# State-space mixer: the two directions' decays added before one masked product, with dt as a logarithm in the exponent

## What is computed

```
dt = softplus(dt_raw + dt_bias)           # per position, direction and head
log_a = dt * -exp(a_log)
v_f, v_b = xh * dt_f, xh * dt_b
# in a chunk, j the position written, l the position read, cs = cumsum(log_a):
y_intra = sum_l (q_j . k_l) * exp(cs_j - cs_l)[j >= l] * v_l      # forward; backward alike with j < l
y_inter = (q_j . h) * exp(cs_j)           # h: the state that the other chunk leaves
y = y_forward + y_backward + xh * d_skip
y = rms_norm_by_group(y * silu(z)) * norm_g @ w_out
```

## Time and profile before

| what | value |
|---|---|
| median of 3 runs | 1048.15 us (1047.29 to 1057.39) |
| profiled execution | 1050.53 us |
| its span, first to last instruction | 1048.7 us |
| mean granted TensorE clock | 0.987 of full speed |
| PE busy | 999.6 us, 95% |
| POOL busy | 693.2 us, 66% |
| ACT busy | 621.7 us, 59% |
| DVE busy | 490.1 us, 47% |

### The profile page before, as it was taken

How to read it: one execution, slowest core, us unless ns; L and a number is a source line. 1 busy time by engine, 2 the same in 40 slices (tenths; PEclk the granted TensorE clock), 3 DMA queues, 4 the chain that set the end, 5 groups by cost and what they waited for, 6 DMA issues and landing times. The chain is left out here.

```text
span 1048.7 us, 16332 instructions
## 1 busy us (share of the span) xinstructions
PE 999.6 (95%) x6297; PEld 879.0 (84%) x6297; DVE 490.1 (47%) x996; ACT 621.7 (59%) x1143; POOL 693.2 (66%) x548
## 2 busy tenths in 40 slices
PE   5999999999999889999999899999989999999988
PEld 4898779999999788988878799999977887787776
DVE  3745344435344466686744544444353143223453
ACT  7636656555546676686766664554565558755621
POOL 3977617765677686677667657575679756766654
PEclk9999999999999999999989999999999999999989
DMA  9774415765554565653744455646445755544311
GB/s 330 237 205 161 132 72 185 249 229 199 180 184 134 162 204 151 211 177 105 241 136 160 146 171 191 201 161 201 162 161 178 193 161 183 181 140 140 110 52 41
DMA packets 131947, 178.71 MB, mean 170 GB/s; under 512 B 21457, under 2 KB 94045, under 8 KB 131677
## 3 DMA queue, kind: packets, MB, share of 16 engines
q1 hardware_dynamic: 127693, 169.95, 50.3%
q10 hardware_dynamic: 4176, 7.71, 2.1%
HBM read 176.51 MB, written 5.24 MB: 173 GB/s over the span
## 5 line engine op out<-in xcount | busy, mean ns | idle before, releaser
L509 POOL TENSOR_TENSOR wlo<-raw,whi 128x512 fp32r<-128x512 f32 x512 | 671.9, 1348 | 331.5 <-ACT whi L1180 325.1
L526 PE MATMUL PS<-Th,whi 128*128 128x256 f32 (+2 forms) x1016 | 290.4, 286 | 3.5 <-DVE Tl L1699 2.8
L528 PE MATMUL PS<-Th,wlo 128*128 128x256 f32 (+2 forms) x1016 | 287.2, 283 | 0.0
L527 PE MATMUL PS<-Tl,whi 128*128 128x256 f32 (+2 forms) x1016 | 287.1, 283 | 0.0
L1180 ACT ACTIVATE whi<-raw 128x1024 fp32r<-128x1024 f32 (+1 forms) x149 | 156.0, 1047 | 178.9 <-PE PS L528 128.1
L523 PE MATMUL PS<-whi,Th 128*128 128x512 f32 (+1 forms) x512 | 206.5, 403 | 10.1 <-DVE Tl L1699 4.2
L1772 DVE SCALAR_TENSOR_TENSOR arena<-PS,cols,arena 128x255 f32<-128x255 f32 (+1 forms) x272 | 118.7, 478 | 189.4 <-ACT arena L1309 165.6
L526 PEld LDWEIGHTS PS<-Th,whi 128*128 128x128 f32 (+2 forms) x1016 | 194.5, 191 | 9.6 <-issue 5.6
L525 PE MATMUL PS<-whi,Tl 128*128 128x512 f32 (+1 forms) x512 | 199.3, 389 | 0.0
L524 PE MATMUL PS<-wlo,Th 128*128 128x512 f32 (+1 forms) x512 | 199.2, 389 | 0.0
L527 PEld LDWEIGHTS PS<-Tl,whi 128*128 128x128 f32 (+2 forms) x1016 | 194.5, 191 | 1.7 <-issue 0.7
(11 more groups left out here) (228 smaller groups left out, 1076.3 us busy)
## 6 DMA issues: line engine op xcount, KB each, us to landing
raw<-in_ffn_w_up_dram SPq DMA_DIRECT2D x44, 1024.0 KB, 5.1
raw<-in_ffn_w_down_dram SPq DMA_DIRECT2D x22, 1024.0 KB, 4.9
raw<-in_w_in_dram SPq DMA_DIRECT2D x22, 1024.0 KB, 5.0
raw<-in_c_w_in_dram SPq DMA_DIRECT2D x16, 1024.0 KB, 5.4
raw<-in_ab_w_in_dram SPq DMA_DIRECT2D x14, 1024.0 KB, 6.2
raw<-in_c_w_out_dram SPq DMA_DIRECT2D x8, 1024.0 KB, 5.3
raw<-in_ab_w_out_dram SPq DMA_DIRECT2D x4, 1024.0 KB, 4.9
raw<-in_c_w_in_dram SPq DMA_DIRECT2D x8, 512.0 KB, 5.4
```

The lines of the kernel that those rows point to most:

```text
L509: i = nc.gpsimd.tensor_tensor(wlo[n % NLO][:, c:e], raw[n % NRAW][:, c:e], whi[n % NHI][:, c:e].bitcast(F32), ALU.subtract)
L526: mm(o, wh, ah, start=first, stop=False)
L527: mm(o, wh, al, start=False, stop=False)
L528: return mm(o, wl, ah, start=False, stop=last)
```

## The change

One product does for both directions. Written as j and l above, forward and backward exclude each other, so the two decays can be added first, and x can stay without dt once log(dt) is in the exponent. In particular:

- `lnd` is the logarithm of dt, clamped at 1e-37 (one VectorE and one ScalarE instruction more, at the start). `ncs`, the bias of the exponentials, was minus the sum and becomes `lnd` minus the sum: four VectorE instructions where ScalarE had one.
- `vx` is x alone, 2 copies a group, in place of `vfb`, 4 products a group.
- The forward exponentials go to `ef` in SBUF, the backward ones to banks 4 and 5. `masked` runs for 4 units w (chunk and half) instead of 8: an add in the bank, then the product.
- `diag` runs for 4 units: 16 products a group instead of 32. Those of chunk 0 stand between slots 3 and 4, those of chunk 1 after slot 4. `T_lo` of the group before is waited for ahead of chunk 0.
- The turned result goes to banks 6 and 7 in every group, and slot 3 waits no more for its reading.
- SyncE issues the rows of units 4 to 7 all ahead of slot b + 7 (6 and 7 were ahead of b + 8), and GpSimd selects them all ahead of slot b + 5 (6 and 7 were ahead of b + 6).
- ScalarE's order changes: units 0, 2, then `T_hi`, 1, 3, the centre tap of the next group's `xs` without the slot that followed it, 4, 5, one slot, 6, 7, then Silu; the next slot comes after Silu.
- VectorE's order follows, with the convolution of the next group ahead of units 2 and 3.

```diff
-            for u, k, m in ((0, 5, 4), (2, 5, 4), (4, 7, 5), (6, 8, 6)):
+            for u, k, m in ((0, 5, 4), (2, 5, 4), (4, 7, 5), (6, 7, 5)):
...
         def turn_bank(g):
-            return 0 if g < SG - 2 else 6
+            return 6
...
-                def diag(u):
-                    c, r, hf = u // 4, (u // 2) % 2, u % 2
-                    pe.wait_ge(*at("s_m", (g, u)))
+                def diag(w):
+                    c, hf = w // 2, w % 2
+                    pe.wait_ge(*at("s_m", (g, w)))
                     for k in range(4):
                         h = 4 * hf + k
-                        i = mm(PS[:, 7 - c, h * DH:(h + 1) * DH], dec[u % 2][:, k, :], vfb[:, r, c, h * DH:(h + 1) * DH],
-                               start=u % 4 == 0 and k == 0, stop=False, skip_group_check=True)
+                        i = mm(PS[:, 7 - c, h * DH:(h + 1) * DH], dec[w % 2][:, k, :], vx[:, c, h * DH:(h + 1) * DH],
+                               start=w % 2 == 0 and k == 0, stop=False, skip_group_check=True)
...
-                pair(0)
-                ssd_slot(g + 1, 3, mid=lambda: pair(2))
-                pair(4)
+                def tile_diag(c):
+                    if g and not c:
+                        pe.wait_ge(*at("T_lo", (("y", g - 1), 3)))
+                    diag(2 * c)
+                    diag(2 * c + 1)
+
+                ssd_slot(g + 1, 3)
+                tile_diag(0)
+                ssd_slot(g + 1, 4)
+                tile_diag(1)
                 if last:
-                    ssd_slot(g + 1, 4)
-                    pair(6)
                     ssd_slot(g + 1, 5, mid=lambda: last_turn(0))
                     last_turn(1)
-                else:
-                    ssd_slot(g + 1, 4, mid=lambda: pair(6))
...
-                    if u >= 2:
-                        act.wait_ge(*at("s_m", (g, u - 2)))
+                    if c:
+                        act.wait_ge(*at("s_m", (g, hf)))
                     for k in range(4):
                         a = ncs_at[(c, r)] + 8 * g + 4 * hf + k
-                        i = act.activation(PS[:, 4 + u % 2, k * P:(k + 1) * P], crow[v % 4][:, k, :], ACT.Exp, bias=ncs[:, a:a + 1])
+                        o = PS[:, 4 + hf, k * P:(k + 1) * P] if r else ef[hf][:, k, :]
+                        i = act.activation(o, crow[v % 4][:, k, :], ACT.Exp, bias=ncs[:, a:a + 1])
...
+                if g == 0:
+                    act.wait_ge(*at("ncs"))
                 exps(0)
-                exps(1)
+                exps(2)
...
-                exps(2)
+                exps(1)
                 exps(3)
                 if more:
-                    ssd_centre(g + 1, 1)
+                    ssd_centre(g + 1, 1, False)
                 exps(4)
                 exps(5)
                 high(b + 5)
                 exps(6)
                 exps(7)
-                high(b + 6)
                 if more:
                     ssd_silu(g + 1)
                 else:
+                    high(b + 6)
                     last_root(0)
...
+            act.wait_ge(*at("la"))
+            act.activation(lnd, lnd, ACT.Ln).then_inc(*done("lnd"))
             act.wait_ge(*at("cums"))
             act.activation(dtt[:, 8:10, :], PS[:, 6, 0:128].rearrange("p (a b) -> p a b", a=2), ACT.Exp).then_inc(*done("ex"))
-            act.activation(ncs, PS[:, 6, 64:192], ACT.Copy, scale=-1.0).then_inc(*done("ncs"))
...
-                    for r in range(2):
-                        i = tt(hb(vfb[:, r, t, :]), hb(PS[:, 4 + t, :]),
-                               bc(dtt[:, t, 32 * r + 8 * g:32 * r + 8 * g + 8], 2, DH), ALU.mult)
+                    nc.vector.tensor_copy(vx[:, t, :], PS[:, 4 + t, :])
...
+                def masked(w):
+
+                    c, hf = w // 2, w % 2
+                    v = PS[:, 4 + hf, :].rearrange("p (a b) -> p a b", a=4)
+                    dve.wait_ge(*at("s_e", (g, 4 * c + 2 + hf)))
+                    dve.wait_ge(*at("s_e", (g, 4 * c + hf)))
+                    lk(tt(v, v, ef[hf][:, :, :], ALU.add))
...
+                    tt(dec[hf][:, :, :], v, bc(qk[:, c, :], 1, 4), ALU.mult).then_inc(*done("s_m", (g, w)))
...
                 masked(0)
-                masked(1)
                 if g:
                     T_lo(("y", g - 1), 4, (4 + 4 * g) % 16, turn_bank(g - 1), lambda k: col("ssdn", 4 * g - 4 + k))
-                masked(2)
-                masked(3)
+                masked(1)
                 dve.wait_ge(*at("s_yie", g))
                 for c in range(NT):
                     i = tt(y[:, c, :], y[:, c, :], xs[g % 2][:, c, :], ALU.add)
                 lk(i)
-                masked(4)
-                masked(5)
                 if more:
                     ssd_conv(g + 1, 1)
+                masked(2)
+                masked(3)
                 ssd_tile(g, 0)
-                masked(6)
-                masked(7)
```

More of the change, by code:

```diff
@@ L321, in build @@
         btm = view(5120, NT, P)
-        vfb = view(5376, 2, NT, 512)
+        vx = view(5376, NT, 512)
+        ef = [view(6400 + 512 * i, 4, P) for i in range(2)]
+        lnd = view(6400, 128)
         vt = view(7424, 2, 512)
@@ L895, in ssd_slot @@
                         pe.wait_ge(*read((("z", g - 1), 1)))
-                    if g >= 2:
-                        pe.wait_ge(*at("T_lo", (("y", g - 2), 3)))
-                    slot_tm((("z", g), 0), 0, 0, True, False, mid=mid)
+                    slot_tm((("z", g), 0), 0, 0, True, False, mid=mid, mid_at=3)
                 else:
@@ L925, in turned_x @@
                     pe.wait_ge(*at("cv", (g, 1)))
-                    pe.wait_ge(*(at("s_m", (g - 1, 7)) if g else read((("z", 0), 1))))
+                    pe.wait_ge(*(at("s_m", (g - 1, 3)) if g else read((("z", 0), 1))))
                     for t in range(NT):
@@ L959, in ssd @@
                 ssd_slot(g + 1, 2, mid=(lambda: ssd_turn(g - 1)) if g else None)
-                if last:
-                    pe.wait_ge(*at("T_lo", (("y", g - 1), 3)))
-                def diag(u):
-                    c, r, hf = u // 4, (u // 2) % 2, u % 2
-                    pe.wait_ge(*at("s_m", (g, u)))
+                def diag(w):
+                    c, hf = w // 2, w % 2
+                    pe.wait_ge(*at("s_m", (g, w)))
                     for k in range(4):
                         h = 4 * hf + k
-                        i = mm(PS[:, 7 - c, h * DH:(h + 1) * DH], dec[u % 2][:, k, :], vfb[:, r, c, h * DH:(h + 1) * DH],
-                               start=u % 4 == 0 and k == 0, stop=False, skip_group_check=True)
[L970 to L974, removed]
-                pair(0)
-                ssd_slot(g + 1, 3, mid=lambda: pair(2))
-                pair(4)
+                        i = mm(PS[:, 7 - c, h * DH:(h + 1) * DH], dec[w % 2][:, k, :], vx[:, c, h * DH:(h + 1) * DH],
+                               start=w % 2 == 0 and k == 0, stop=False, skip_group_check=True)
+                    i.then_inc(*done("s_pv", (g, w)))
+                def tile_diag(c):
[7 more added lines that the diff above has]
+                tile_diag(1)
                 if last:
-                    ssd_slot(g + 1, 4)
-                    pair(6)
                     ssd_slot(g + 1, 5, mid=lambda: last_turn(0))
                     last_turn(1)
-                else:
-                    ssd_slot(g + 1, 4, mid=lambda: pair(6))
             def run_sums():
@@ L1456, in _, with ssd_centre @@
             act.dma_start(dtt[:, 6, 0:32], I["c_d_skip"].to_broadcast([P, 32])).then_inc(*done("load_ssd", 0, 16))
-            def ssd_centre(g, j):
-                used(((("xs", g), j) if j < 2 else (("bc", g), 0)))
+            def ssd_centre(g, j, ahead=True):
+                used(((("xs", g), j) if j < 2 else (("bc", g), 0)), ahead)
                 for m in range(2):
@@ L2001, in ssd_tile @@
                 y = hn[:, c, (g % 2) * 512:(g % 2) * 512 + 512]
-                dve.wait_ge(*at("s_pv", (g, 4 * c + 3)))
+                dve.wait_ge(*at("s_pv", (g, 2 * c + 1)))
                 i = tt(y, y, PS[:, 7 - c, :], ALU.add)
@@ L2029, in ssd @@
                     dve.wait_ge(*at("ex"))
+                    dve.wait_ge(*at("lnd"))
+                    for c in range(NT):
+                        for r in range(2):
+                            a = ncs_at[(c, r)]
+                            i = tt(ncs[:, a:a + 32], lnd[:, 64 * c + 32 * r:64 * c + 32 * r + 32], PS[:, 6, 64 + a:96 + a], ALU.subtract)
+                    i.then_inc(*done("ncs"))
                     tt(dtx[:, 0:32], dtt[:, 0, 0:32], exv[:, 0:32], ALU.mult)
@@ L2053, in ssd @@
                 i.then_inc(*done("s_yie", g))
-                def masked(u):
-                    c, r, hf = u // 4, (u // 2) % 2, u % 2
-                    dve.wait_ge(*at("s_e", (g, u)))
-                    if u >= 2:
-                        dve.wait_ge(*at("s_pv", (g, u - 2)))
+                def masked(w):
[4 more added lines that the diff above has]
+                    lk(tt(v, v, ef[hf][:, :, :], ALU.add))
```

(8 more changed lines are left out.)

## The result

The changed kernel takes 1035.57 us, median of 4 runs (1034.44 to 1038.97), against 1048.33 us for the kernel before in the same comparison: a ratio of 0.9881, 95% interval 0.9859 to 0.9903, so 12.8 us less. The forecast was 1034.5 us in a range of 1027 to 1044. A second comparison gave 1035.56 us and 0.9874 (0.9858 to 0.9890). The profiled execution took 1034.44 us; its mean granted clock was 0.992 of full speed. In a stretch, 1.00 means that TensorE ran at the higher of its two levels (2.4 GHz) throughout, 0.50 at the lower one (1.2 GHz); values between are mixtures of the two.

A forecast was written before the change was run, and what follows sets the result against it. TensorE, busy 95%, was taken to bound the kernel, with ScalarE's chain next. Start -1.1, group 0 +3.7, groups 1 and 2 +8.0, group 3 +4.4 gave 15.0 us less: 1034.5 us, range 1027 to 1044.

The forecast's parts named there:

- What bounds it: Whole mixer: TensorE, busy 95%, bounds the kernel; ScalarE sets what comes next once TensorE has less to do.
- 13.6 us of TensorE's own work goes: Products within a chunk: 8 of 16 runs of 1.70 us go; how much arrives depends on the chain beside it.
- Start: Start of the section: added logarithm and two more table loads on ScalarE make it 1.1 us late, bounds 0 and 2.8.
- Groups 1 and 2: ScalarE's chain through Silu sets a period of 39.4 us: 4.0 us gained in each, 0.8 to 0.9 us new waiting.
- Group 0: First group: ScalarE's chain is covered, TensorE alone sets a period of 36.6 us, 3.7 us gained.
- rival 2: New waits let TensorE's clock fall to half: 1043.8 us with three falls, 1038 to 1041.6 with one or two; chance 0.24.
- Group 3: Last group to the last turn: slot 3 covers the old wait and clock fall; last turn at 567.3, 4.4 us gained.
- A full clock in group 3: Sign to look for: full clock in group 3, with 1 to 2 us of waiting ahead of the last run.
- 3.55 of it the clock: Group 3: 3.55 us of the 4.4 us gain come from work no longer run at half clock after the 1.98 us wait.
- Moved at no cost: VectorE's copies, slot b + 7's later load and ScalarE's slot behind Silu cost nothing; uncovered, up to 4 us a group.
- rival 4: Weights come late: slot b + 7's later load reaches TensorE with 3.9 us in three groups, 1046 us; chance 0.05.
- Rival 3: Late row transfers for units 5 to 7 make it slower: at 7.2 us everywhere, with half clock, 1060 us; chance 0.04.

The follow-up runs named there:

- Experiment 1: Kernel before with 1 of 4 products of each backward unit issued (48 of 128 left out): 1047.78 us against 1048.50 us, ratio 0.9992.
- experiment 6: Changed kernel with units 5 and 6 exchanging row buffers, so unit 5's rows wait for unit 2 instead of unit 1: 1032.06 us, ratio 0.9845.
- experiment 8: Changed kernel with, in group 3 alone, ScalarE's slot b + 4 ahead of the first exponentials: 1031.35 us, ratio 0.9847.
- Experiment 2: Changed kernel with each of its 64 products within a chunk issued twice: 1040.38 us, ratio 0.9924.
- experiment 7: Changed kernel with a_log's exponential ahead of softplus's logarithm and row buffers exchanged: 1038.07 us; then also clamped dt in a bank: 1035.14 us, ratio 0.9870.
- experiments 5 and 6 together: Changed kernel with a_log's exponential ahead of softplus's logarithm and units 5 and 6 exchanging row buffers: 1038.07 us, ratio 0.9907.
- experiment 10: Kernel before with slot 3 of group 3 put ahead of that group's first products: 1047.72 us, ratio 1.0006.
- experiment 3: Changed kernel with rows of units 6 and 7 requested and selected one slot later, as before: 1064.17 us, ratio 1.0166.

## Why the prediction was right, and where it missed

**What bounds it: right.** The prediction said that ScalarE sets what comes next once TensorE has less to do. Experiment 1 shows this even for the old order, experiments 6 and 8 for the new one. Yet "13.6 us of TensorE's own work goes" sounds like the source of the gain. Experiment 2 puts the halved count at 4.8 us once the order is new, experiment 1 puts three quarters of it at 0.7 us in the old one.

**Start: right.** 1.1 us were charged; the section starts 1.34 us later, of which 0.25 us was there before the added instructions. Both table loads are there, at 382.66 and 384.28. The Trainium skill, "ScalarE: Activation LUTs", section "Table sets: the hidden batching unit", would have had one set for both functions; these two rows contradict it for this program. Of the VectorE instructions that were charged nothing, or 0.8 us if late, the clamp took 1.08 us, in a place where 9 us is possible (experiment 7). That it cost nothing hangs on a gap in GpSimd's work, which the prediction had not looked at. The adds with both ends in a bank did not cost twice their neighbour, but the same: 0.70 us at 547.93 for an add, 0.69 us at 548.67 for the product behind it.

**Groups 1 and 2: right, and for the stated reason.** Counted from the group's start (431.64 in the walk, 431.36 in the changed kernel), unit 5 was forecast 30.8 us in and came 30.8 us in; the end of Silu was forecast at 39.3 and came at 39.3; the period at 39.4 and came at 39.30 and 39.73. The new waits were forecast at 0.8 to 0.9 us. The waits of TensorE at the end of group 1 are 0.23, 0.26 and 0.21 us, in sum 0.7. Removing the cause (experiment 6) brings 38.16 and 38.73 us, about what was forecast for TensorE alone.

**Group 0: the size was off.** Forecast 3.7 us, came 1.6. The step that failed is the assumption that the 3.10 us wait would again be followed by a full clock. In the profiled execution before, the clock behind it was 1.00; in the changed kernel 0.66, and the eight turns took 1.94 us where they had taken 1.06. This is rival 2, in one place. Where the clock held, the forecast period did too. In the kernel of experiments 5 and 6 together, where the wait ahead was 2.57 us, the stretch was

```profile
398.00:406.00 8.00, 7.83 (x59) 7.25 (x60) 4.01 (x7) 0.03 (x1) 3.18 (x3) 1.00 1.03 290
```

and group 0 took 36.52 us against 36.6 forecast. The prediction had counted the 3.10 us wait as evidence against rival 2. It wasn't: in the kernel of experiment 1, whose program is that of before up to this place, the same wait was followed by a clock of 0.60 (its stretch above). Over all profiled executions of this case, twelve have this wait of 3.10 us; in the 8 us from the turn's start the clock was 1.00 in two of them, those of the kernel before and of experiment 10, and 0.63 to 0.80 in the other ten. The one profile at hand was one of the two.

**Group 3: the size was off, and the source of the gain was wrong.** Forecast 4.4 us, came 2.8. The step that failed is the start of the walk. It took the first half of the group at its old length, but the turn of the result, which had come 537.13 - 518.35 = 18.78 us into the group, came 530.52 - 510.39 = 20.13 us in, 1.35 us later, at a granted clock of 1.00. TensorE in the kernel before, then ScalarE and TensorE in the changed kernel:

```profile
537.13 1.03 PE L609 MATMUL PS<-cst,hn 128*128 128x128 f32 x8
...
512.14 1.06 ACT L1347 ACTIVATE arena<-PS 128x512 f32<-128x512 f32 x2
...
513.25 0.50 PE L525 MATMUL PS<-whi,Th 128*128 128x512 f32 x1 [0.55 <-ACT arena L1347]
...
530.52 1.03 PE L611 MATMUL PS<-cst,hn 128*128 128x128 f32 x8
```

L1347 is ScalarE's copy of the turned x. It now stands behind Silu and the slot that was moved behind Silu, and begins 1.75 us into the group where it began 0.20 us in; TensorE waits 0.55 us for it, and 0.33 us for VectorE shortly before. In experiment 2 TensorE reaches this place later and waits for neither: the turn of the result comes 18.85 us in, and group 3 is 1.24 us shorter. A further 0.5 us comes from the selections of units 4 and 5, at 2.15 us for two (experiment 8) where about 0.6 us was counted ahead of unit 4. So the last exponential ended 38.6 us into the group where 36.8 us were forecast. A wait of 1.82 us ahead of the last run was forecast at 1.5, and the tail went as forecast, with 12.0 us from the last exponential to the last turn for 12.2.

"A full clock in group 3" was wrong as well: behind that wait the clock was 0.66. But this is not where the time went. The last run in the kernel of experiment 6, and its second half in that of experiments 5 and 6 together:

```profile
546.21 3.54 PE L970 MATMUL PS<-arena 128*128 128x64 f32 x16 [1.83 <-DVE arena L2075]
...
551.33 1.10 PE L970 MATMUL PS<-arena 128*128 128x64 f32 x8 [0.22 <-DVE arena L2076]
```

The first ran at half clock and took 3.54 us, the second at a granted clock of 1.00, with 2.4 us for the whole run; group 3 took 50.41 and 50.37 us. The last turn waits for VectorE in both, 0.33 and 0.96 us. Likewise "3.55 of it the clock" was no source of gain: experiment 10 gives that back and the time stays. By experiments 3 and 10, what shortens such a group is that units 6 and 7 are selected ahead of a slot's low part and not behind it.

**Moved at no cost: right for the loads, not for ScalarE's slot.** No wait for weights of the later load appeared; rival 4 fell. ScalarE's slot behind Silu did cost, in group 3, through the copy that now follows it. Rival 3 fell: no row took over 5.8 us. In rival 2's price the prediction mixed two bases: its 1043.8 us for three falls starts from the median and the 1038 to 1041.6 us from the forecast, by which three falls would be 1045.2 us. That the sum came so near, 1034.5 for 1035.6, has a part of luck: the section gave only 10.7 us of the 15.0 in the profiled pair, and 1048.3 - 10.7 would be 1037.6 us. The other 2 us between the medians lie outside the walk or in executions that have no profile.

**Open.** Why the same wait of 3.1 us is followed by half clock in most executions and not in all; where the falls of TensorE's clock behind the section come from; how long GpSimd can hold a VectorE instruction; and what the single table load at the start is worth in the whole time, beyond the 1.1 us in its place.

## What to carry to other kernels

With an engine at 95%, ask first who stands less than a microsecond behind it, since work taken from it is worth only that much until the order of the suppliers is changed too. Give out buffers in the order in which they come free along the slowest chain; that took 1.7 to 2.1 us off two periods here, and 3.5 us off the median. A stall or a half clock ahead of another late supplier is worth nothing until that supplier has been moved. And when an engine's work is moved behind another piece, look at what else stood behind that place.

## What the hardware showed that was not expected

- A VectorE instruction from SBUF to SBUF beside an unbroken run of GpSimd took 8.97 us and ended with that run; 1.08 us where it began 0.3 us behind a gap of 0.69 us, although GpSimd's run then went on for 8.7 us; 0.29 us with its result in a bank.
- A wait of 3.10 us ahead of the same instructions was followed by a granted clock of 1.00 over 8 us in two executions and of 0.63 to 0.80 in ten. Where TensorE alone decides, the lower clock costs some 2 us (group 0 took 38.67 us behind that wait, and 36.52 us at 1.00 behind a wait of 2.57 us); where a supplier decides, it cost nothing (group 3 took 50.41 us at half clock and 50.37 us at full clock).
- An exponential of 128x128 took 394 ns into SBUF and 355 ns into a bank on average, but four in a row 1.29 and 1.24 us: they overlap, and the forward exponentials' move to SBUF cost nearly nothing.
